# A chunked scan on one core: the wide product of a level signals twice, and ScalarE's first copy waits for the first signal

## The reference, cut to what matters

```python
def step(S, inp):
    w_t, k_t, v_t, kk_t, b_t = inp[:5]
    sa = jnp.einsum('bhvk,bhk->bhv', S, kk_t)
    S = (S * w_t[:, :, None, :] - sa[..., None] * b_t[:, :, None, :]
         + v_t[..., None] * k_t[:, :, None, :])
    o = jnp.einsum('bhvk,bhk->bhv', S, inp[5]) if with_out else None
    return S, o
...
S, o = lax.scan(step, S0, xs, reverse=reverse)
```

## Time and profile before

| | us |
|---|---|
| median of 3 runs | 4689.36 |
| lowest and highest | 4686.57 and 4690.65 |
| the profiled execution, its own time | 4687.34 |
| its span, first to last instruction | 4685.6 |
| the scan in it, about 1376 to 2612 | 1236 |

### The profile page before, as it was taken

One profiled execution on the slowest core, in us unless ns is written; L12 is line 12 of the kernel. 1 busy time (PEld: TensorE's weight loads), 2 busy tenths in 40 slices (PEclk: granted clock), 3 DMA queues, 4 the chain that ended last, 5 costly groups with the idle time before them and its releaser, 6 DMA issues. The chain is left out here.

```text
span 4685.6 us, 66517 instructions
## 1 busy us (share of the span) xinstructions
PE 4531.5 (97%) x27608; PEld 3671.8 (78%) x27608; DVE 2674.1 (57%) x3938; ACT 1728.0 (37%) x2924; POOL 457.7 (10%) x371
## 2 busy tenths in 40 slices
PE   7999999999999999999999799899998789999999
PEld 4888877778999888988898444688777567888887
DVE  3245544555636676767677676546453755555543
ACT  3234444444424544554445343211343742111111
POOL 0000000000012233322334100000010000000000
PEclk8999999999999999999999999999999999999999
DMA  5244343434430110111012343333120021212222
GB/s 207 99 144 148 134 144 138 145 139 148 160 115 15 45 57 30 59 45 59 28 59 86 90 150 120 128 107 134 54 71 15 23 113 59 72 68 77 99 90 95
DMA packets 155978, 441.79 MB, mean 94 GB/s; under 512 B 17168, under 2 KB 47120, under 8 KB 140448
## 3 DMA queue, kind: packets, MB, share of 16 engines
q1 hardware_dynamic: 140624, 383.98, 23.5%
q0 software_dynamic: 9296, 32.58, 2.0%
q10 hardware_dynamic: 5760, 20.97, 1.2%
HBM read 294.86 MB, written 141.56 MB: 93 GB/s over the span
## 5 line engine op out<-in xcount | busy, mean ns | idle before, releaser
L202 PE MATMUL pr_ps<-uhl,w_split 128*128 128x512 f32 (+1 forms) x1520 | 586.9, 386 | 3.1 <-DVE w_split L145 2.2
L206 PE MATMUL pr_ps<-uhl,w_split 128*128 128x512 f32 (+1 forms) x1520 | 571.7, 376 | 0.0
L205 PE MATMUL pr_ps<-uhl,w_split 128*128 128x512 f32 (+1 forms) x1520 | 571.1, 376 | 0.0
L1581 DVE TENSOR_TENSOR b_G<-b_ps,cst 128x512 fp32r<-128x512 f32 x560 | 383.2, 689 | 95.4 <-PE b_ps L1361 93.7
L138 ACT ACTIVATE w_split<-share 128x2048 fp32r<-128x2048 f32 x64 | 122.6, 1916 | 698.9 <-DVE ou_vc L3303 271.1
L202 PEld LDWEIGHTS pr_ps<-uhl,w_split 128*128 128x128 f32 x1520 | 287.0, 189 | 81.7 <-issue 29.2
L205 PEld LDWEIGHTS pr_ps<-uhl,w_split 128*128 128x128 f32 x1520 | 287.3, 189 | 56.3 <-issue 5.8
L206 PEld LDWEIGHTS pr_ps<-uhl,w_split 128*128 128x128 f32 x1520 | 286.9, 189 | 52.8
L1124 POOL TENSOR_SCALAR b_Mr<-b_tri 128x512 fp32r<-128x512 f32 x80 | 117.8, 1490 | 1908.7 <-DVE b_tri L1565 1908.7
L202 PE MATMUL ou_ps<-ou_a,w_split 128*128 128x512 f32 x704 | 276.5, 393 | 7.7 <-DVE ou_a L2158 7.7
L1361 PE MATMUL b_ps<-b_G,b_EY 128*128 128x128 f32 x1600 | 275.4, 281 | 0.0
(11 more groups left out here) (498 smaller groups left out, 10030.2 us busy)
## 6 DMA issues: line engine op xcount, KB each, us to landing
w_ring<-in_w_in SPq DMA_DIRECT2D x41, 1024.0 KB, 5.3
proj<-pr_stage SPq DMA_DIRECT2D x160, 256.0 KB, 2.0
share<-in_w_up SPq DMA_DIRECT2D x24, 1024.0 KB, 4.8
ar<-share SPq DMA_DIRECT2D x32, 512.0 KB, 2.8
b_AR<-ar SPq DMA_DIRECT2D x64, 256.0 KB, 2.9
pr_raw<-proj SPq DMA_DIRECT2D x48, 256.5 KB, 3.5
ada<-in_ada_w SPq DMA_DIRECT2D x24, 512.0 KB, 5.6
ff<-ou_vc ACTq DMA_DIRECT2D x24, 512.0 KB, 2.6
```

The lines of the kernel that those rows point to most:

```text
L202: mm = nc.tensor.matmul(dst, a[0], b[0], start=start, stop=False)
L205: nc.tensor.matmul(dst, a[0], b[1], start=False, stop=False)
L206: return nc.tensor.matmul(dst, a[1], b[0], start=False, stop=stop)
L1581: L[x]["dve"].done(V.tensor_tensor(Gs[x][m % 2][:], heads(x, 0 if m else 1), rep(K(f"lev{m}"), 4), ALU.mult), f"{n}.G{m}")
```

## The change

The wide product signals twice: a new signal `lo{m}` on the second matmul, when bank 1 is full, and `EY{m}` on the fourth as before. ScalarE's `low` waits for `lo{m}`. For direction 0 its `high` gets a wait of its own, on `EY{m}`. VectorE's `high_out` keeps its wait on `EY{m}`. No instruction is added and none changes its place; one matmul of four gets one more increment, and one activation of three a wait.

```diff
         def level_names(n, x):
-            return {"pe": ["F0", "E0"] + sum(([f"F{m}", f"EY{m}"] for m in range(1, 5)), []) + ["F5", "Y5", "Y6"],
+            return {"pe": ["F0", "E0"] + sum(([f"F{m}", f"lo{m}", f"EY{m}"] for m in range(1, 5)), []) + ["F5", "Y5", "Y6"],
...
                 def ey_out(i, n, x, m):
-                    L[x]["pe"].wait(act, i, f"{n}.EY{m}")
+                    L[x]["pe"].wait(act, i, f"{n}.lo{m}")
                     L[x]["act"].done(A(EY[x][:, 0:2], both(x)[:, 0:2], ACT.Copy), f"{n}.low{m}")
                     if not high_on_dve(x):
+                        L[x]["pe"].wait(act, i, f"{n}.EY{m}")
                         L[x]["act"].done(A(EY[x][:, 2:4], both(x)[:, 2:4], ACT.Copy), f"{n}.high{m}")
...
                     for q in range(4):
                         mm = mmul(both(x)[:, q], Gs[x][m % 2][:, q], EY[x][:, q], start=True, stop=True)
-                    L[x]["pe"].done(mm, f"{n}.EY{m}")
+                        if q % 2:
+                            L[x]["pe"].done(mm, f"{n}.{'lo' if q == 1 else 'EY'}{m}")
```

## The result

The changed kernel takes 4652.36 us, the median of 5 runs (4649.09 to 4654.19). The kernel before, in 5 runs beside it, takes 4686.57 (4685.37 to 4690.65). The ratio is 0.9925, with a 95% interval of 0.9914 to 0.9937: 34.2 us less. The forecast was 4654.4 and 35.0 us less. It was counted from 4689.4, the median of the first three runs of before, and the two later ones were lower; so the gain is the fairer comparison.

The account below looks back on a forecast made before the run. The prediction took a 2.14 us loop through direction 0's ScalarE copies as the bound; 146 passages x 0.24 us = 35.0 us, off 4689.4, gave 4654.4 us. Forecast band 4650 to 4659 (0.68), range 4644 to 4668.

Parts of the forecast that it names:

- What bounds the kernel: Scan level: loop of wide product, low copy, high copy, F's third load, next wide product, 2.14 us; 0.30 is wait.
- TensorE's own pace: Rival: each scan level falls to 1.84 us, four groups at 0.46; gain 43.8 us, so 4645.6; chance 0.08.
- The earlier first copy: Direction 0's low copy waits for two matmuls, starts 0.24 us earlier; loop 1.90 us against 2.14.
- How often: Passages between scan levels: 160, of which 14 behind 512-column matmuls gain nothing and 146 gain.
- The sum: Whole kernel: 146 x 0.24 = 35.0 us less, 4689.4 to 4654.4 us.
- Is anything else late then?: Other engines in a level: VectorE tight at 1.84 us under 1.90, margins 0.08 and 0.15; nothing else late.
- The extra signal and wait: 320 more matmul increments and the high copy's own wait: cost taken as 0, bounds 0.24 and -0.02 us.
- increments adding up in the signal: Rival: low copy starts 0.03 us later than reckoned; gain 30.7 us, so 4658.7; chance 0.07.
- VectorE's loop: Rival: VectorE's three operations, 2.14 us a level, set the pace: 4672 in part (0.08), 4689 wholly (within a shared 0.05).
- no effect: Rival: a mid-group matmul's signal comes out only with its group; 4689; chance within a shared 0.05.
- slower: Rival: increments inside a group break TensorE's pipelining, 0.24 us each, level pace 2.32; 4722; chance 0.04.
- The gain kept whole: Rest of each unit and stages after the scan: they move along, so none of the 35.0 us is lost.

Follow-up runs that it names:

- third_matmul: Changed kernel with the first signal on the wide product's third matmul instead of the second, low copies waiting for it: 4668.89 us, ratio 0.9965 to before.
- split_high: Changed kernel with direction 0's high copy in two, E columns (all F needs) first, then Y columns: 4645.58 us, ratio 0.9914 to before.
- dir0_only: Changed kernel, but only direction 0's low copy waits for the first signal, direction 1's for the second: 4656.25 us, ratio 0.9938 to before.
- split_high_on_before: Kernel before, one signal for each wide product, with only direction 0's high copy in two, E columns first: 4665.74 us, ratio 0.9957 to before.
- signal_only: Changed kernel with both signals of the wide product, but every copy still waits for the second: 4685.91 us, ratio 0.9998 to before.
- four_signals: Changed kernel with an increment on each of the wide product's four matmuls, copies waiting for the second and fourth as there: 4652.22 us, ratio 0.9928 to before.

## Why the prediction was right, step by step

- *What bounds the kernel.* Right. The loop closed to 2.14 from rows of before, and each change of the low copy's signal moved the level by what it took out of the loop: 0.12 (third_matmul), 0.23 (changed); split_high took out more and stopped at 0.30, at TensorE's own pace. What the prediction doesn't have is the second loop, through the low copy alone, at 1.94. It played no part in the change itself, which shortens it in both directions, but it decided dir0_only and split_high_on_before.
- *The earlier first copy*: 1.90 forecast, 1.91 measured; low copy 0.54 forecast, 0.55 measured; low to high 0.49 instead of 0.50; F's loads span 0.60 as forecast.
- *How often*: 146 passages. The sum, 146 x 0.24 = 35.0, came out 34.2 in the medians and 33.8 in the stretch, which holds 145 of them (it ends at the last wide product). The 14 passages with 512-column matmuls took 3.56 us on the mean in both kernels, so they gained nothing, as forecast. The term that was a little off is 0.24: the medians of all levels are 2.140 and 1.906, so 0.234. Loads had given 0.23, ends of matmuls 0.24, and I took the ends; the loads were the better reading. 145 x 0.234 is 33.9.
- *Is anything else late then?* VectorE was the tight one, and it was on time: its high copy of direction 1 ends at 1984.63 + 0.68 = 1985.31, and F of direction 1 behind it (1985.21) spans 0.53, so its third load didn't wait. G of direction 0 (L1583) starts at 1983.32, where VectorE comes free and not where F ends, as forecast, and cost nothing.
- *The low copy of direction 1* I passed over with one sentence, that it follows the high copy "and gets 0.24 earlier with it". That is true for the change, where it too waits for the first signal. But it hides that this half of the edit carries 6 us; dir0_only showed it.
- *The extra signal and wait*: 0 forecast, 0 shown by signal_only and four_signals. Four increments leave the low copy where two put it, 0.548 us after the first load as a median in both. The Trainium skill, "TensorE: Matmul & The Clock Gate", section "The cost: per-tile semaphore tail", states 26.3 ns for each increment, for the tiles of a matmul array that is split up. To carry that over to these matmuls, which fill the array and start 0.11 to 0.12 us apart one after the other, was the prediction's own step, and the traces show no such cost here.
- *The rivals.* TensorE's own pace was not reached by the change (that took split_high). VectorE's loop, increments adding up in the signal, no effect and slower didn't come.
- *The gain kept whole*: yes. The rest of the unit moved along and the stages outside the scan differ by -2.2 and +1.9 us.

## What to carry to other kernels

Where a long pass of matmuls feeds a copy that feeds the next pass, look for the loop and add it up from the starts of weight loads; a TensorE that reads 99% busy held a stall of 0.30 us in each level of 2.14 here. A signal for each bank as it fills takes the remaining matmuls out of the loop, here at no cost that level or time shows, and each matmul taken out was worth its own pace of 0.11 to 0.12 us. Add up the shorter loops too (here 1.94 behind 2.14): the next one sets the pace as soon as the longest is cut. And cut both of two interleaved chains, even if one of them shows no gain alone: its lateness grows inside the levels and comes out where they end.

## What the runs showed of the hardware

- Matmul increments 0.12 us apart showed no cost: 320 more than before leave the level at 2.14, 960 more than in the changed kernel leave it at 1.91, and the time stays within its interval in both.
- Weight loads followed a copy that they waited for at a fixed distance: F's third load 0.049 to 0.053 us behind the end of ScalarE's high copy (before, 146 passages), F's first load 0.112 to 0.114 behind the end of the low copy (before and dir0_only).
- ScalarE copied bank 1 while TensorE wrote bank 2 of the same direction: the copy took 601 ns on the mean against 600 before, and the four loads of the wide product still span 0.54 us.
- Stages that are the same in every kernel here differ between profiled executions by up to 10 us. From the last wide product's load to the end it is 4681.9 - 2596.6 = 2085.3 us in signal_only, at a mean granted clock of 0.987 over the whole span, and 4648.1 - 2552.7 = 2095.4 in split_high, at 0.983. That is more than the 6 us that separate split_high from the changed kernel in the medians, and so for edits of this size the stretch that holds the edit is the better measure.
